# A two-network forward pass on one core: the latent attention's prelude taken block by block, its shared rope key computed as 64 extra columns of the query latent, and the squares of the feed-forward's first groups placed ahead of weight splits

## Chip, cores and metric

The kernel runs on one core of a Trainium2 chip. The metric is the device time of one execution in microseconds (us); lower is better.

## What is computed

Two small networks run one after the other on x of shape 256 x 1024 in float32. The first has a short-convolution mixer and a multi-head latent attention (MLA), each followed by a squared-ReLU feed-forward, all with layer norms; the second a gated linear recurrence and a block attention. The part around the change, shortened:

```python
cq = _rms_norm(x @ w_dq, g_q)                       # 256 x 384, the query latent
q = (cq @ w_uq).reshape(bsz, seq, MLA_HEADS, QK_NOPE + QK_ROPE)
ckv_full = x @ w_dkv                                # 256 x 320
ckv = _rms_norm(ckv_full[..., :KV_LORA], g_kv)      # 256 x 256, the key and value latent
k_pe = _rope(ckv_full[..., None, KV_LORA:], cos, sin)[:, :, 0, :]   # 64 wide, shared by 8 heads
k_nope = jnp.einsum("bsc,chd->bshd", ckv, w_uk)
v = jnp.einsum("bsc,chd->bshd", ckv, w_uv)
...
s = (q_nope . k_nope + q_pe . k_pe) * scale, masked; softmax; times v; @ w_o
...
_sq_relu_mlp: jnp.square(jax.nn.relu(x @ w1)) @ w2  # 1024 -> 4096 -> 1024
```

## The kernel before

**Weights.** Every weight matrix is cut into pieces of at most 128 x 2048 floats (`piece_table`). SyncE's queue (SP) loads them one after another into a ring of three raw buffers (`RAW`), and a load starts when VectorE (DVE) has finished with the piece three places back (`raw_done`). ScalarE (ACT) rounds a piece to the high half (`w_high`, L908), DVE subtracts to get the low half (`w_low`, L1206), both into a ring of six (`RING`); TensorE (PE) then makes each product of three matmuls: high x high, high x low, low x high. `split_ahead(key, n)` on ACT and on DVE carries this on up to n pieces past the piece `key`; where it stands in an engine's program fixes what is queued behind it. Between the weight pieces of a feed-forward lie "mod" pieces of the second network's modulation: DVE accumulates each in eight steps (L1218, L1221), POOL adds the two halves (L862), PE sums over partitions (`mod_sums`, L615), DVE reads the result (`read_mod`, L1231).

**Feed-forward** (`feed_forward`, one function per engine; ff0 and ff1). There are 16 groups of 256 hidden columns; group g is an up product, relu on ACT (L971), the square on DVE (L1348), and two down products, one per block of 128 tokens (b = 0, 1). The first three groups (`FILL`) are made token-major, block 0 first, so that they can begin while block 1's layer norm is still under way: PE runs `up_block(g, 0)` for g = 0, 1, 2, then for each g `up_block(g, 1)` and, from g = 1, `turn(g - 1)`, four transposes that wait for the square of group g - 1 (L533). Then `mod_sums`, the down products of group 0, turn(2), `mod_sums`, and the first feature-major up product, up(3) (L482). On DVE before the change each group starts with `split_ahead((phase, "up", g), AHEAD)`, and the square comes behind it.

**Prelude of the latent attention** (`latents`, L1446 to L1515 on DVE). For each block, PE makes the key-value latent (24 matmuls of 256 columns, piece dkv) and the query latent (24 of 384, pieces dq). The shared rope key is a product of its own: piece kpe holds the 64 columns and their halves exchanged, each twice, and `feature_block` (L510 to L512) multiplies it feature-major, 48 matmuls of 128 columns per block. Block 0's half stands behind the transposes of x's block 1, block 1's half behind the transposes of the key latent (tkv). DVE normalises both blocks of a latent in one go, PE transposes it, DVE applies the gain, ACT and DVE make its high and low half. Then follow keys, the turned query latent, keys, values (`across`), and the attention loop: for each pair of heads the projections qn and qp (36 matmuls of 256 columns), scores (L656, L659), softmax, values. POOL makes the reciprocal roots (L854, L855). Products go through three PSUM banks in the order of `unit_table`; a bank is reopened once it is emptied (`await_evacuated`).

Of the kernel before, what the change touches and what calls it, by code (L numbers as in the profile page):

```python
# [18 lines left out]
ALU = mybir.AluOpType  # L19
# [37 lines left out]
def piece_table():  # L57
# [81 lines left out]
def unit_table():  # L139
# [3 lines left out]
    def attention(phase, projections):  # L143
        for g in range(MXG + 1):
            if g < MXG:
                t.extend((phase, kind, g) for kind in projections)
            if phase == "mo" and g == MXG:
# [7 lines left out]
    t.extend([("mla", "tkv"), ("mla", "kpe"), ("mla", "k", 0), ("mla", "k", 1)])  # L155
    t.extend([("mla", "tq", 0), ("mla", "tq", 1), ("mla", "k", 2), ("mla", "k", 3)])
    t.extend(("mla", "v", b, n) for b in range(TB) for n in range(2))
# [36 lines left out]
def last_unit(phase, kind, n):  # L194
# [5 lines left out]
    return {"kpe": ("mla", "kpe"), "uk": ("mla", "k", 3), "uv": ("mla", "v", 1, 1),  # L200
# [4 lines left out]
LAYER_NORMS = {"ln0": TB, "ln1": TB, "latent": 2, "ln2": TB, "ln3": TB}  # L205
SQUARES = {"rs1": TB, "rs2": TB, "rs3": TB}

ROOTS = {"ln0": TB, "ln1": TB, "latent": 2, "ln2": TB, "ln3": 2 * TB, "rs2": TB, "rs3": TB}
# [51 lines left out]
def build(nc, weights, x_in, cols_in, consts_in, rows_in, out):  # L260
    with ExitStack() as ctx:
# [87 lines left out]
        gain_in, shift_in = sem("gain_in"), sem("shift_in")  # L349
        ones_ready, c_tanh, lam_exp_in, lam_exp = sem("ones_ready"), sem("c_tanh"), sem("lam_exp_in"), sem("lam_exp")  # L350
        prm_ready, diag_ready = sem("prm_ready"), sem("diag_ready")
        lora_ready, lora_high, lora_low, rope_ready = sem("lora_ready"), sem("lora_high"), sem("lora_low"), sem("rope_ready")
# [47 lines left out]
        area_v = area_f.rearrange("p (b n) -> p b n", b=TB)  # L400
        q_all = flat(rows).rearrange("p (h s) -> p h s", s=SEQ)
# [12 lines left out]
        def _(sp):  # L414
# [7 lines left out]
            for s, (kind, n) in enumerate(STREAM):  # L422
# [7 lines left out]
                if s == RAW:  # L430
                    sp.dma_start(consts[:, P:], consts_in[:, P:]).then_inc(consts_in_done, 16)
# [19 lines left out]
        def _(pe):  # L451
# [47 lines left out]

            def feature_block(dst, n, b, fresh):  # L500

                await_piece(n)
                for tile in range(GT):
                    o = dst[:, tile * SEQ + b * P:tile * SEQ + (b + 1) * P]
                    for kt in range(KT):
                        if tile == 0 and kt % 4 == 0:
                            await_xT(fresh, b, kt // 4)
                        c = (tile * KT + kt) * P
                        high, low = w_high[:, n % RING, c:c + P], w_low[:, n % RING, c:c + P]
                        mm(o, high, xT_h[:, kt, tok(b)], start=kt == 0, stop=False)  # L510
                        mm(o, high, xT_l[:, kt, tok(b)], start=False, stop=False)
                        last = mm(o, low, xT_h[:, kt, tok(b)], start=False, stop=kt == KT - 1)  # L512
                return last
# [198 lines left out]
            def latents(b):  # L712

                for q in range(2):
                    await_xT("ln1", b, q)
                i = PI["mla", "dkv", 0]
                await_piece(i)
                token_major(Y[b][1][:, 0:KV_LORA], i, KT, KV_LORA, 0, KV_LORA, b, xT_h, xT_l, True, True).then_inc(latent, 1)
                for n in range(2):
                    i = PI["mla", "dq", n]  # L720
                    await_piece(i)
                    last = token_major(Y[b][0][:, 0:Q_LORA], i, KT // 2, Q_LORA, 0, Q_LORA, b, xT_h[:, 4 * n:4 * n + 4, :],
                                       xT_l[:, 4 * n:4 * n + 4, :], n == 0, n == 1)
                last.then_inc(latent, 1)

            latents(0)
# [990 lines left out]
```

## Time and profile before

| | |
|---|---|
| median of 3 runs | 889.57 us (887.39 to 889.62) |
| profiled execution, its own time | 888.67 us |
| its span in the trace | 886.9 us |
| PE busy | 819.4 us, 92% of the span |
| DVE, ACT, POOL busy | 619.5, 402.1, 156.3 us |
| mean granted TensorE clock | 0.963 |
| moved by DMA | 174.38 MB, mean 197 GB/s |

The span is what the trace covers; the execution's own time is 1.8 us longer. Durations below are from this one profiled execution. In the trace ff0 begins at about 107 us, the prelude at 304.95, the attention's first score at 349.00, and ff1 at about 417. A matmul's duration in the trace overlaps its neighbours', so PE's pace is read from starts. The granted clock is 1.00 at 2.4 GHz and 0.50 at 1.2 GHz.

### The profile page before, as it was taken

The page shows a single profiled execution, that of the slowest core. Times are in us where ns is not written, and L with a number is a line of the kernel's source. Part 1 is how long each engine was busy: PE and PEld are TensorE (multiplying, and loading weights), DVE is VectorE, ACT ScalarE, POOL GpSimd, SP SyncE. Part 2 cuts the span into 40 slices and gives each one's busy share as a digit, 9 for nine tenths or more (in the row PEclk, how much of TensorE's full clock was granted, in tenths as well). Part 3 has the DMA queues.
Part 4 walks back from the last instruction along what each step waited for, and adds up shares of the span by engine and source line. Part 5 has one row for each costly group of instructions (what it writes and reads, how often), then busy time and mean ns, then how long its engine had stood idle before and what let it go on. Part 6 is the DMA issues. An engine that isn't in the chain of part 4 may idle for free.

```text
span 886.9 us, 13139 instructions
## 1 busy us (share of the span) xinstructions
PE 819.4 (92%) x5410; PEld 751.0 (85%) x5410; DVE 619.5 (70%) x941; ACT 402.1 (45%) x469; POOL 156.3 (18%) x86
## 2 busy tenths in 40 slices
PE   6999979999999999999799999997778969979985
PEld 6999878999999897878789999996778959979974
DVE  6776887777777766766877777776477775546643
ACT  5443244434344235561544444343567874454531
POOL 0110012233443000000123344331300002020000
PEclk9999999999999999999999999999798988999998
DMA  7974456877776324333568777762043443734101
GB/s 294 346 284 161 173 196 250 315 283 285 274 272 241 141 72 168 141 143 143 213 241 310 280 285 281 263 244 90 25 167 130 193 171 115 276 137 144 48 25 47
DMA packets 25691, 174.38 MB, mean 197 GB/s; under 512 B 2848, under 2 KB 3104, under 8 KB 6176
## 3 DMA queue, kind: packets, MB, share of 16 engines
q1 hardware_dynamic: 25632, 173.54, 53.4%
q8 instruction: 43, 0.70, 0.3%
q14 instruction: 16, 0.13, 0.0%
HBM read 172.48 MB, written 1.05 MB: 196 GB/s over the span
## 4 chain that ended last, share of the span: by engine, by line
PE 80%; DVE 9%; ACT 6%; DMA 2%; issue 2%; POOL 0%; POOLq 0%; ACTq 0%; SPq 0%; DVEq 0%
PE bank L482 13%; PE bank L484 12%; PE bank L483 12%; PE Y L580 10%; PE Y L581 9%; PE Y L583 9%; DVE w_low L1206 3%; ACT w_high L908 2%; DMA raw<-weights 1%; PE mbank L615 1%; PE Y L606 1%; PE Y L656 1%; PE bank L544 1%; PE bank L545 1%; PE bank L546 1%
## 5 line engine op out<-in xcount | busy, mean ns | idle before, releaser
L1206 DVE TENSOR_TENSOR w_low<-raw,w_high 128x2048 fp32r<-128x2048 f32 (+2 forms) x130 | 287.0, 2227 | 57.0 <-ACT w_high L908 56.4
L482 PE MATMUL bank<-xT_h,w_high 128*128 128x256 f32 x928 | 270.3, 291 | 16.8 <-DVE xT_l L1302 7.2
L908 ACT CAST w_high<-raw 128x2048 fp32r<-128x2048 f32 (+2 forms) x130 | 239.4, 1854 | 80.5 <-DMA raw<-weights 70.9
L483 PE MATMUL bank<-xT_l,w_high 128*128 128x256 f32 x928 | 266.3, 287 | 0.0
L484 PE MATMUL bank<-xT_h,w_low 128*128 128x256 f32 x928 | 266.0, 287 | 0.0
L482 PEld LDWEIGHTS bank<-xT_h,w_high 128*128 128x128 f32 x928 | 181.6, 196 | 18.7 <-issue 8.0
L483 PEld LDWEIGHTS bank<-xT_l,w_high 128*128 128x128 f32 x928 | 181.8, 196 | 0.4 <-issue 0.2
L484 PEld LDWEIGHTS bank<-xT_h,w_low 128*128 128x128 f32 x928 | 181.7, 196 | 0.0
L580 PE MATMUL Y<-w_high,hT_h 128*128 128x512 f32 x344 | 136.7, 397 | 0.2 <-DVE hT_l L1237 0.2
L581 PE MATMUL Y<-w_low,hT_h 128*128 128x512 f32 x344 | 135.5, 394 | 0.0
L583 PE MATMUL Y<-w_high,hT_l 128*128 128x512 f32 x344 | 107.8, 395 | 0.0
L862 POOL TENSOR_TENSOR macc<-macc 128x256 f32<-128x256 f32 x16 | 61.3, 3832 | 153.3 <-DVE macc L1221 153.3
L862 POOL TENSOR_TENSOR stage<-stage 128x256 f32<-128x256 f32 x16 | 63.5, 3970 | 134.5 <-DVE stage L1221 134.5
L971 ACT ACTIVATE buf_a<-bank 128x512 f32<-128x512 f32 x32 | 19.1, 598 | 131.0 <-PE bank L484 124.4
L583 PEld LDWEIGHTS Y<-w_high,hT_l 128*128 128x128 f32 x344 | 65.2, 189 | 14.3
L580 PEld LDWEIGHTS Y<-w_high,hT_h 128*128 128x128 f32 x344 | 65.7, 191 | 13.1 <-DVE hT_l L1237 0.7
L581 PEld LDWEIGHTS Y<-w_low,hT_h 128*128 128x128 f32 x344 | 65.4, 190 | 13.2
L854 POOL TENSOR_SCALAR small<-small 128x1 f32<-128x1 f32 (+1 forms) x16 | 7.1, 444 | 390.7 <-DVE small L1263 171.3
L1348 DVE SCALAR_TENSOR_TENSOR buf_b<-bank,buf_a 128x512 f32<-128x512 f32 x32 | 22.1, 690 | 58.0 <-ACT buf_a L971 58.0
L920 ACT CAST hT_h<-buf_b 128x512 fp32r<-128x512 f32 x34 | 21.1, 620 | 53.1 <-DVE buf_b L1445 28.3
L1221 DVE SCALAR_TENSOR_TENSOR stage<-raw,cs,stage 128x256 f32<-128x256 f32 x96 | 39.4, 480 | 0.0
L1221 DVE SCALAR_TENSOR_TENSOR macc<-raw,cs,macc 128x256 f32<-128x256 f32 x96 | 39.3, 479 | 0.0
(196 smaller groups left out, 1129.3 us busy)
## 6 DMA issues: line engine op xcount, KB each, us to landing
raw<-weights SPq DMA_DIRECT2D x152, 1024.0 KB, 5.1
rows<-rows_in SPq DMA_DIRECT2D x9, 512.0 KB, 7.1
raw<-weights SPq DMA_DIRECT2D x6, 768.0 KB, 4.3
raw<-weights SPq DMA_DIRECT2D x4, 512.0 KB, 4.6
x<-x_in SPq DMA_DIRECT2D x2, 512.0 KB, 4.1
out<-x SPq DMA_DIRECT2D x2, 512.0 KB, 2.7
consts<-consts_in SPq DMA_DIRECT2D x1, 320.0 KB, 5.3
cols<-cols_in SPq DMA_DIRECT2D x1, 118.5 KB, 6.4
```

The lines of the kernel that those rows point to most:

```text
L482: mm(dst, high, xh[:, kt, :], start=kt == 0, stop=False)
L483: mm(dst, high, xl[:, kt, :], start=False, stop=False)
L484: last = mm(dst, low, xh[:, kt, :], start=False, stop=kt == kts - 1)
L580: mm(Y[b][h][:, :], th[:, t0 + t, tok(b)], high[h], start=first, stop=False)
L581: mm(Y[b][h][:, :], th[:, t0 + t, tok(b)], low[h], start=False, stop=False)
L583: last = mm(Y[b][h][:, :], tl[:, t0 + t, tok(b)], high[h], start=False, stop=final)
L862: nc.gpsimd.tensor_tensor(acc[:, 0, :], acc[:, 0, :], acc[:, 1, :], ALU.add).then_inc(mod_added, 1)
L908: nc.scalar.copy(w_high[:, n % RING, start:COLS[n]], raw[:, s % RAW, start:COLS[n]]).then_inc(w_high_ready, 1)
L920: nc.scalar.copy(hT_h[:, t0:t0 + GT, :], src).then_inc(hidden_high, 1)
L1206: tt(w_low[:, n % RING, start:COLS[n]], slot[:, start:COLS[n]], f32(w_high[:, n % RING, start:COLS[n]]), ALU.subtract).then_inc(raw_done, 1)
L1221: step = stt(out=acc, in0=part, scalar=cs[:, kt:kt + 1], in1=acc, op0=ALU.mult, op1=ALU.add)
L1348: squared = stt(out=buf_b[:, g % 2, :], in0=bank_of(phase, g)[:, :], scalar=0.0, in1=buf_a[:, g % 2, :], op0=ALU.max, op1=ALU.mult)
```

## The change

Three parts.

1. **Rope key.** Piece kpe and `feature_block` go. The 64 rope columns are appended to the query latent's weights: the dq pieces are 4 x (384 + 64) columns, and their matmuls 448 wide. DVE turns the key token-major from PSUM (`rope_key`, five small operations per block, with cos and sin per token that one more DMA puts into buf_a), PE transposes it (one transpose per block), ACT copies it.
2. **Prelude by block.** Norm, transposes, gain, high and low half are made per block and interleaved with the latent products; values of block 0 come ahead of the keys, values of block 1 behind the first projections; the piece uv comes before uk.
3. **Feed-forward, groups 0 to 2, in ff0 and ff1.** On DVE and ACT the splits come behind the relu and square of the group; at group 1 only the mod piece is accumulated there, and the two weight pieces wait for group 2.

```diff
     for n in range(2):
-        add("mla", "dq", n, KT // 2 * Q_LORA)
-    add("mla", "kpe", 0)
+        add("mla", "dq", n, KT // 2 * (Q_LORA + ROPE))
+    add("mla", "uv", 0)
     add("mla", "uk", 0)
-    add("mla", "uv", 0)
...
+                if key == ("mla", "uk", 0):
+                    await_evacuated(sp, "ff0", FFG - 1)
+                    sp.dma_start(buf_a[:, 1, 2 * P:], consts_in[:, 2 * P + 2 * SEQ:]).then_inc(key_turn_in, 16)
...
+            latent_kv(0)
+            latent_q(0, 0)
+            transposes("ln1", x, "x_ready", [1])
+            latent_q(0, 1)
+            latent_kv(1)
+            turn_latent("tkv", 0)
+            latent_q(1, 0)
+            turn_latent("tq", 0)
+            latent_q(1, 1)
+            turn_latent("tkv", 1)
+            pe.wait_ge(lora_low, 1)
+            latent_values(0)
+            pe.wait_ge(lora_low, 3)
+            for n in range(4):
+                up(PI["mla", "uk", 0], ("mla", "k", n), 2 * n, CT, *ckv)
+                if n == 1:
+                    turn_latent("tq", 1)
+                    dst = open_unit("mla", "kpe")
+                    for b in range(TB):
+                        pe.wait_ge(kpe_ready, b + 1)
+                        last = nc.tensor.transpose(dst[:, tok(b)], macc[:, b, P:2 * P], ident)
...
             def project(g):
+                if g == 0:
+                    pe.wait_ge(lora_low, 4)
                 for i, kind in enumerate(("qn", "qp")):
                     up(PI["mla", "q", g], ("mla", kind, g), GT * i, QT, hT_h, hT_l)
+                if g == 0:
+                    latent_values(1)
...
             def feed_forward(phase, m0):
                 for g in range(FFG):
-                    split_ahead((phase, "up", g), AHEAD if g else AHEAD - 1)
+                    if g == 0 or g >= FILL:
+                        split_ahead((phase, "up", g), AHEAD if g else AHEAD - 1)
...
+                    if g < FILL:
+                        split_ahead((phase, "up", 0 if g < FILL - 1 else g), AHEAD, min(g, 1) if g < FILL - 1 else 0)
```

**DVE, groups 0 and 1 of ff0** (L1348, after the change L1372, is the square; L1206 and L1226 a weight's low half; raw to stage a mod piece). Before:

```order
L1348 SCALAR_TENSOR_TENSOR buf_b<-bank,buf_a 128x512 [waits relu]
L1206 TENSOR_TENSOR w_low<-raw,w_high 128x2048 [waits w_high_ready]
L1218 TENSOR_SCALAR stage<-raw,cs 128x256 [waits mod_summed,raw_in0]
L1218 TENSOR_SCALAR stage<-raw,cs 128x256
L1221 SCALAR_TENSOR_TENSOR stage<-raw,cs,stage 128x256 [waits dve_chain] x6
L1206 TENSOR_TENSOR w_low<-raw,w_high 128x2048 [waits w_high_ready]
L1348 SCALAR_TENSOR_TENSOR buf_b<-bank,buf_a 128x512 [waits relu]
L1252 TENSOR_TENSOR hT_l<-bank,hT_h 128x512 [waits hidden_high]
```

After the change:

```order
L1372 SCALAR_TENSOR_TENSOR buf_b<-bank,buf_a 128x512 [waits relu]
L1226 TENSOR_TENSOR w_low<-raw,w_high 128x2048 [waits w_high_ready]
L1372 SCALAR_TENSOR_TENSOR buf_b<-bank,buf_a 128x512 [waits relu]
L1272 TENSOR_TENSOR hT_l<-bank,hT_h 128x512 [waits hidden_high]
L1238 TENSOR_SCALAR stage<-raw,cs 128x256 [waits mod_summed,raw_in0]
L1238 TENSOR_SCALAR stage<-raw,cs 128x256
L1241 SCALAR_TENSOR_TENSOR stage<-raw,cs,stage 128x256 [waits dve_chain] x6
L1251 TENSOR_TENSOR modcol<-mbank,cols 128x2 [waits mod_summed]
```

Two weight splits stood between the squares of groups 0 and 1, with a mod piece between them; one split stands there now, and the mod piece follows the second square.

**PE, the transposes of x's block 1 in the prelude** (L606, now L596; x_ready is the layer norm's signal). Before, the rope key's first matmuls follow, with a wait for the transposed block:

```order
L606 MATMUL Y<-consts,x 128x128 [waits x_ready]
L606 MATMUL Y<-consts,x 128x128 x3
L606 MATMUL Y<-consts,x 128x128 [waits x_ready]
L606 MATMUL Y<-consts,x 128x128 x3
L510 MATMUL bank<-xT_h,w_high 128x128 [waits xT_low,raw_done,evacuated2]
L511 MATMUL bank<-xT_l,w_high 128x128
```

After the change:

```order
L536 MATMUL Y<-w_high,xT_l 128x448
L596 MATMUL Y<-consts,x 128x128 [waits x_ready]
L596 MATMUL Y<-consts,x 128x128 x3
L596 MATMUL Y<-consts,x 128x128 [waits x_ready]
L596 MATMUL Y<-consts,x 128x128 x3
L534 MATMUL Y<-w_high,xT_h 128x448 [waits raw_done]
```

What follows the transposes is the second half of block 0's query latent, which waits for its weights alone.

**DVE, the key-value latent's norm and gain** (BN_STATS to the reciprocal root's operand, then the normalised latent buf_b, then the gain from a PSUM bank). Before, in one go for both blocks:

```order
L1462 BN_STATS small<-Y 128x6 [waits latent] x2
L1465 BN_AGGR small<-small 128x2 [waits dve_chain]
L1465 BN_AGGR small<-small 128x2
L1467 TENSOR_TENSOR small<-small 128x2 [waits dve_chain]
L1468 TENSOR_TENSOR small<-small 128x2 [waits dve_chain]
L1474 TENSOR_SCALAR buf_b<-Y,small 128x256 [waits rstd_ready]
L1474 TENSOR_SCALAR buf_b<-Y,small 128x256
L1492 TENSOR_SCALAR stage<-bank,cols 128x256 [waits product]
L1492 TENSOR_SCALAR stage<-bank,cols 128x256
```

After the change, block 0's part (L1330 makes x's low half of block 1, L1226 splits the piece uk):

```order
L1482 BN_STATS small<-Y 128x6 [waits latent]
L1483 BN_AGGR small<-small 128x2 [waits dve_chain]
L1484 SCALAR_TENSOR_TENSOR small<-small 128x1 [waits dve_chain]
L1330 TENSOR_TENSOR xT_l<-Y,xT_h 128x4x128 [waits xT_high] x2
L1491 TENSOR_SCALAR buf_b<-Y,small 128x256 [waits rstd_ready,consts_in_done]
L1226 TENSOR_TENSOR w_low<-raw,w_high 128x2048 [waits w_high_ready]
L1482 BN_STATS small<-Y 128x6 [waits latent]
L1483 BN_AGGR small<-small 128x2 [waits dve_chain]
L1484 SCALAR_TENSOR_TENSOR small<-small 128x1 [waits dve_chain]
L1499 TENSOR_SCALAR buf_b<-bank,cols 128x128 [waits product]
L1499 TENSOR_SCALAR buf_b<-bank,cols 128x128
```

A latent's steps for block 0 now stand ahead of, and between, the steps for block 1.

## Rows read from the trace of the kernel before

**Rows 1.** The page of the profile, part 1 (busy time of PE) and part 4 (the chain).
```profile
PE 819.4 (92%) x5410; PEld 751.0 (85%) x5410; DVE 619.5 (70%) x941; ACT 402.1 (45%) x469; POOL 156.3 (18%) x86
...
PE 80%; DVE 9%; ACT 6%; DMA 2%; issue 2%; POOL 0%; POOLq 0%; ACTq 0%; SPq 0%; DVEq 0%
```

**Rows 2.** PE's waits: line, what was waited for: us in total, times, longest us.
```profile
PE bank L533 <- DVE buf_b L1348: 11.8, 2, 6.4
```

**Rows 3.** Timeline of PE, start of ff0: start us, us, engine, line, operation, tiles.
```profile
131.77 1.11 PE L533 MATMUL bank<-consts,buf_b 128*128 128x128 f32 x4 [6.44 <-DVE buf_b L1348]
...
140.93 0.36 PE L482 MATMUL bank<-xT_h,w_high 128*128 128x256 f32 x1
```

**Rows 4.** Timeline of DVE and ACT, start of ff0 (idle before and its releaser in brackets).
```profile
128.82 2.29 DVE L1206 TENSOR_TENSOR w_low<-raw,w_high 128x2048 fp32r<-128x2048 f32 x1 [2.03 <-ACT w_high L908]
131.03 0.68 DVE L1348 SCALAR_TENSOR_TENSOR buf_b<-bank,buf_a 128x512 f32<-128x512 f32 x1
...
126.89 1.90 ACT L908 CAST w_high<-raw 128x2048 fp32r<-128x2048 f32 x1 [5.32 <-DMA raw<-weights]
```

**Rows 5.** Stretches: us, busy of PE, PEld, DVE, ACT, POOL; granted clock; DMA share; GB/s.
```profile
130.00:135.00 5.00, 3.23 (x12) 2.94 (x13) 5.00 (x6) 2.65 (x3) 0.00 (x0) 0.50 0.75 264
349.00:354.88 5.88, 5.88 (x17) 3.16 (x17) 5.84 (x5) 0.00 (x0) 0.00 (x0) 0.66 0.53 189
354.88:360.42 5.54, 5.54 (x38) 5.54 (x38) 2.80 (x13) 3.79 (x10) 0.00 (x0) 0.74 0.96 356
362.95:367.03 4.08, 4.08 (x19) 2.27 (x17) 3.83 (x11) 1.50 (x5) 0.00 (x0) 1.00 0.48 147
367.03:371.24 4.21, 4.21 (x38) 4.21 (x38) 1.95 (x9) 3.02 (x8) 0.00 (x0) 1.00 0.27 111
```

**Rows 6.** Timeline of PE, start of ff1.
```profile
441.24 1.11 PE L533 MATMUL bank<-consts,buf_b 128*128 128x128 f32 x4 [5.41 <-DVE buf_b L1348]
...
450.94 0.36 PE L482 MATMUL bank<-xT_h,w_high 128*128 128x256 f32 x1
```

**Rows 7.** Timeline of PE: a turn, and two down products with their modulation sum.
```profile
121.86 0.60 PE L533 MATMUL bank<-consts,buf_b 128*128 128x128 f32 x4
122.22 0.36 PE L523 MATMUL bank<-w_high,xT_h 128*128 128x256 f32 x1
...
456.78 0.39 PE L580 MATMUL Y<-w_high,hT_h 128*128 128x512 f32 x1
...
462.27 0.50 PE L615 MATMUL mbank<-ones,stage 128*128 128x1 f32 x4
462.64 0.36 PE L482 MATMUL bank<-xT_h,w_high 128*128 128x256 f32 x1
```

**Rows 8.** The two stretches in which PE computes the shared rope key.
```profile
312.94:318.33 5.39, 5.39 (x50) 5.39 (x49) 3.92 (x4) 4.35 (x4) 0.00 (x0) 1.00 0.49 147
325.79:331.18 5.39, 5.39 (x52) 5.39 (x50) 4.07 (x11) 2.00 (x2) 1.26 (x2) 1.00 0.01 3
```

**Rows 9.** Timeline of PE: latents of block 0, its neighbours, the first score.
```profile
304.95 0.28 PE L544 MATMUL Y<-w_high,xT_h 128*128 128x256 f32 x1
...
307.81 0.34 PE L544 MATMUL Y<-w_high,xT_h 128*128 128x384 f32 x1
...
311.98 0.38 PE L606 MATMUL Y<-consts,x 128*128 128x128 f32 x2
...
349.00 0.46 PE L656 MATMUL Y<-kT,rows 128*128 128x128 f32 x2 [1.42 <-issue]
```

**Rows 10.** Timeline of DVE: around POOL's reciprocal root of the key latent.
```profile
322.40 0.16 DVE L1468 TENSOR_TENSOR small<-small 128x2 f32<-128x2 f32 x1
...
323.67 0.88 DVE L1474 TENSOR_SCALAR buf_b<-Y,small 128x256 f32<-128x256 f32 x2 [1.10 <-POOL small L855]
```

**Rows 11.** Timeline of ACT and POOL: a value bank emptied, a modulation sum's first step.
```profile
343.51 0.59 ACT L1046 COPY z<-bank 128x512 f32<-128x512 f32 x1 [0.76 <-PE bank L546]
...
269.60 4.92 POOL L862 TENSOR_TENSOR stage<-stage 128x256 f32<-128x256 f32 x1 [6.77 <-DVE stage L1221]
```

More of the change, by code:

```diff
@@ L755, in _, with turn_latent @@
-            for b in range(TB):
+            def turn_latent(kind, b):
+                src, kts, count = (ckvn, CT, 2 * b + 1) if kind == "tkv" else (cqn, QT, 2 * b + 2)
+                dst = open_unit("mla", kind, b)
+                pe.wait_ge(lora_ready, count)
+                for kt in range(kts):
+                    last = nc.tensor.transpose(dst[:, kt * P:(kt + 1) * P], src[:, b, kt * P:(kt + 1) * P], ident)
+                in_order("mla", kind, b)
+                last.then_inc(product, 1)
@@ L1047, in _ @@
                         .then_inc(evacuates("mla", "v", b, n), 1)
-            split_ahead(("mla", "uv", 0))
+            latent_high("tkv", 0)
+            split_ahead(("mla", "q", 0), 0)
+            latent_high("tq", 0)
+            latent_high("tkv", 1)
+            latent_values(0)
+            keys(0)
+            keys(1)
+            latent_high("tq", 1)
+            await_product(act, "mla", "kpe")
+            nc.scalar.copy(area[:, 4, :], bank_of("mla", "kpe")[:, 0:SEQ]).then_inc(evacuates("mla", "kpe"), 1)
+            keys(2)
+            keys(3)
+            split_ahead(("mla", "q", 2), 0)
             for g in range(MXG + 1):
@@ L1190, in f32, with split_ahead @@
                 return ap.bitcast(F32)
-            def split_ahead(key, ahead=AHEAD):
-                stop = AT["w", min(PI[key] + ahead, len(PIECES) - 1)]
+            def split_ahead(key, ahead=AHEAD, mods=0):
+                stop = AT["w", min(PI[key] + ahead, len(PIECES) - 1)] + mods
+                assert all(kind == "mod" for kind, _ in STREAM[stop - mods + 1:stop + 1])
                 while done[0] <= stop:
@@ L1470, in latent_normed, with latent_squares @@
-            def latent_normed(i, normed, half, width):
-                await_rstd("latent", i)
-                for b in range(TB):
-                    last = ts(normed[:, b, :], Y[b][half][:, 0:width], rstd[:, TB * i + b:TB * i + b + 1], None, ALU.mult)
-                last.then_inc(lora_ready, 1)
-            def rope(n, *key):
+            def latent_squares(i, b):
+                n, src = TB * i + b, Y[b][0][:, 0:Q_LORA] if i else Y[b][1][:, 0:KV_LORA]
+                dve.wait_ge(latent, 2 * b + i + 1)
+                link(nc.vector.bn_stats(stats[:, n, 0:6], src))
+                link(nc.vector.bn_aggr(mv[:, n, :], stats[:, n, 0:6]))
+                stt(out=msq[:, n:n + 1], in0=mv[:, n, 0:1], scalar=mv[:, n, 0:1], in1=mv[:, n, 1:2], op0=ALU.mult, op1=ALU.add)\
+                    .then_inc(S["var_ready"], 1)
@@ new lines, in latent_low, with rope_key @@
+            def latent_low(i, b):
+                dve.wait_ge(lora_high, 2 * b + i + 1)
+                t0, kts, src = (0, QT, stage[:, b, 0:QT * P]) if i else (QT, CT, buf_b[:, 1, b * CT * P:(b + 1) * CT * P])
+                tt(hT_l[:, t0:t0 + kts, tok(b)], src.rearrange("p (t s) -> p t s", t=kts), f32(hT_h[:, t0:t0 + kts, tok(b)]),
+                   ALU.subtract).then_inc(lora_low, 1)
+            def rope_key(b):
+                k, half = Y[b][0][:, Q_LORA:Q_LORA + ROPE], ROPE // 2
+                straight, crossed = macc[:, b, 0:ROPE], macc[:, b, ROPE:2 * ROPE]
+                dve.wait_ge(latent, 2 * b + 2)
+                dve.wait_ge(key_turn_in, 16)
+                tt(straight, k, cos_k[:, b, :], ALU.mult)
+                tt(crossed[:, 0:half], k[:, half:], sin_k[:, b, 0:half], ALU.mult)
+                link(tt(crossed[:, half:], k[:, 0:half], sin_k[:, b, half:], ALU.mult))
+                for n in range(2):
+                    last = tt(macc[:, b, P + n * ROPE:P + (n + 1) * ROPE], straight, crossed, ALU.add)
+                last.then_inc(kpe_ready, 1)
```

216 lines of the change are left out of this document (92 added, 124 removed).

## The prediction

> **What bounds the kernel now.** I read the page first. PE is busy for 92% of the span, and the chain that ended last lies on PE for 80% of it [rows 1]. So two things can shorten the run: less work on PE, and fewer or shorter waits of PE. The waits by line come next: the largest entry in a feed-forward is L533, the turn of a group in the fill, which waited 11.8 us for the square of DVE in two places [rows 2]. The timelines show where.
>
> In ff0 the second turn starts at 131.77 after 6.44 us of idleness [rows 3]. What it waits for is the square of group 1 at 131.03 on DVE, behind a weight split that started at 128.82. That split waited for ACT's high half, and ACT for a load, 5.32 us [rows 4]. The square is a 0.68 us instruction with its inputs ready long before (the relu of group 1 needs only up products that had ended by 121.9 [rows 7]); it is late because of what is queued ahead of it. While PE stood still its clock fell: the granted clock was 0.50 from 130 to 135 [rows 5], that is 1.2 GHz. ff1 repeats it, with 5.41 us of idleness [rows 6].
>
> In the prelude PE never stands still until the first score at 349.00, where it idles for 1.42 us [rows 9]. The prelude is bound by PE's work, and two stretches of 5.39 us are the rope key's product, at full clock with PE busy throughout [rows 8]. Behind the idle 1.42 us the clock fell again: the scores took 5.88 us and the next projections 5.54 us at a mean clock of 0.66 and 0.74, against 4.08 and 4.21 us in the next round at 1.00 [rows 5].
>
> **The change, term by term.** I sum against the profiled execution's own 888.67 us, which lies 0.9 us under the median of 889.57.
>
> *Feed-forward fill, ff0.* DVE's order becomes: square 0 (about 120), one split (its ACT half is no longer behind a relu, and its load was issued long before), square 1, the low half of group 0, the mod piece, square 2, then two splits. A split takes 2.29 us [rows 4], so square 1 ends near 123.5, before PE asks for it at 131.77 - 6.44 = 125.33 [rows 3]. The mod piece then ends near 127, square 2 near 128. From 125.33 PE now runs straight on: turn 0.36 (122.22 - 121.86), modulation sum 0.37, two down products 5.49 (462.27 - 456.78), turn 0.36, sum 0.37 (462.64 - 462.27) [rows 7], so up(3) starts at 132.28 where it started at 140.93 [rows 3]: 8.65 us gained, 6.44 of it the wait and 2.2 the slow clock behind it. *ff1* likewise: 441.24 - 5.41 + 6.95 = 442.78 against 450.94 [rows 6], 8.16 us. What is late next is the second modulation sum: its mod piece ends near 127, and POOL's add took up to 4.92 us [rows 11], so it is there by 132 and is wanted at 131.9; I take 0.3 us of wait over both. The weight splits put off are two, of group 2's round. Their pieces down(1) and up(4) are wanted by PE at about 138 and 144; with loads issued as slots come free they are split by 134. The slack behind the fill hides them; if it were gone each would cost its 2.29 us. Fill terms: 8.65 + 8.16 - 0.3 = 16.5 us.
>
> *Rope key on PE.* Removed: 2 x 5.39 = 10.78 us, 96 matmuls [rows 8]. Added: 48 of the 128x384 matmuls become 448 wide. The pace is (307.81 - 304.95)/24 = 0.119 us at 256 columns and (311.98 - 307.81)/24 = 0.174 at 384 [rows 9], so 64 columns are 0.027 us, times 48 is 1.3 us. Two transposes at (312.94 - 311.98)/8 = 0.12 us [rows 8, 9] are 0.24. All other PE work of the prelude is only moved. Net 9.2 us. These rows give 0.112 us to a kpe matmul of 128 columns, almost what 256 columns cost. The Trainium skill (TensorE: Matmul & The Clock Gate, Back-to-back issue gap) has a sustained pace of about 81 ns at 128 columns. By that figure the 96 removed matmuls were worth 7.8 us and the sum would be 3.0 us less, near 863.6. The trace has this very work and differs, so the rows decide.
>
> *Waits in the prelude.* The 10.8 us also hid things: block 0's half covered the casts of x's block 1, block 1's half the gain and low half of the key latent. Their new covers, from 304.95: the key latent of block 0 takes 2.9 us, half the query latent 2.4, so PE asks for x's block 1 near 310.2; layer norm gives it at 310.7 (DVE is unchanged up to there): 0.4 us of wait. The other half query latent (2.4) and then the reader of x's low half: the casts need about 2 us behind the transposes, just covered. Query latent, block 0: statistics can start only when its second half ends near 313.6 and stand behind a 2.3 us split; then POOL's root, 1.1 us from request to use (323.67 - 322.40 less the instruction) [rows 10], so it is normalised near 319.5, and PE asks at about 319.0: 0.5 us. Keys need block 1's key latent low at about 325.2, and PE gets there at 325.4. The last query latent's low half comes near 331 and is wanted at 332. The rope key leaves DVE near 327 and is wanted at 329. The rope of the first projection (formerly the 1.42 us) is now covered by block 1's values; instead scores wait until ACT has emptied the last value bank, 0.59 us for the copy [rows 11] and 0.06 to start. Sum of new waits 1.6 us, old wait 1.4. So the first score comes 9.2 + 1.4 - 1.6 = 9.0 us earlier against its predecessor, at 340.0 before the fill's gain.
>
> Bounds for the waits: at best the 0.4 and 0.5 vanish, 0.9 us better; at worst each of the four handovers (query latent block 0, keys, last query latent, first score) is a further 1.1 us root or a 2.3 us split late, about 6 us.
>
> *SP and small operations.* SP gets one more wait and one 128 x 256 load, ahead of q's loads; what it waits for (the last square of ff0) is done some 4 us before. The ten small rope operations, about 0.2 us each, lie on DVE in gaps; they are in the times above. DMA moves 0.8 MB less, on nobody's path.
>
> *The clock at the scores.* The wait ahead of them falls from 1.42 to 0.65 us. The slow stretch cost (5.88 - 4.08) + (5.54 - 4.21) = 3.1 us [rows 5]. Between the attention's later rounds PE idles 0.33 us each time and stays at 1.00; 0.65 is nearer to that, so I let the clock stay up. DVE was busy all of the 5.88 us [rows 5] with splits, so softmax then shows by about 0.5 us: 2.6 us gained. Ends: 0 and 3.1.
>
> Sum: 16.5 + 9.0 + 2.6 = 28.1; 888.67 - 28.1 = **860.6 us**.
>
> **Rivals.**
> A. *The clock still falls at the scores.* For it: PE still idles there, amid small matmuls. Against it: the idle time is halved. 888.67 - 25.5 = 863.2. Chance 0.20.
> B. *The latents' chain is late.* The steps DVE, POOL, DVE, PE, DVE, ACT, DVE now run four times, strictly in DVE's order, so one late step delays all behind it. The margins above are 0.2 us at the keys and 1 us at the last query latent. At 4 to 6 us of waits the time is 865 to 867. Chance 0.18.
> C. *The fill's wait only moves.* The splits put off make down(1), up(4) or the next pieces late, as ACT waited 5.32 us for a load [rows 4]. PE would have to be caught before 144 with half of the gain lost: 860.6 + 8.2 = 869. Against it: six microseconds of slack. Chance 0.08.
> D. *Slower.* The rope product kept PE dense; without it the prelude is short groups between transposes and waits, and the clock could sit at 0.50 from the first latent to the first score. All 33.4 us of work would take 33.4 us more: 860.6 + 33.4 = 894. It decides against the change once some 28 us of full-clock work run at half. Against it: the transposes of x at 311.98 stand in a stretch at 1.00. The Trainium skill (same page, Part 4: PE-mode transpose) holds that transposes don't count as activity for the clock as matmuls do, which speaks for it; no row here shows the clock falling at transposes alone. Chance 0.02.
> E. *The change does not act*, since the square would wait for something else, or the removed product was hidden: within 0.3% of 889. The rows above speak against it. Chance 0.01.
>
> **How the numbers follow.** Forecast 0.51, A 0.20, B 0.18, C 0.08, D 0.02, E 0.01. The mean granted clock of the whole run, 0.963, says that some 65 us ran at half; those other low stretches, of 3 us and more, may shift when everything before them moves, by some 2 us either way at each of a few places. So the forecast's own range is 857 to 863.5. The range of 856 to 868 takes in A and most of B and leaves out C, D and E and the tails. 0.3% is 2.7 us, about what a measurement tells from no change. Faster 0.96, same 0.02, slower 0.02.
>
> **What would show it.** Right: PE's waits for the square gone from the list or under 1 us; up(3) of ff0 near 132.3 and the granted clock 1.00 there; from the first latent to the first score 35.0 us, where it was 44.05; scores of the first round in 4.1 us. Wrong: waits of PE at the latents' transposes, keys or projections of over 1 us each (B); PE idle in groups 3 to 5 of ff0 behind a weight split (C); a granted clock of 0.50 inside the prelude (D). The forecast fails as a whole if the distance from up(3) to the end of a feed-forward grows by what the fill gained.

## The result

The changed kernel takes 862.52 us (median of 4 runs, 860.01 to 863.31), the kernel before 889.6 beside it (4 runs, 887.39 to 891.24). The ratio is 0.9692 with a 95% interval of 0.9663 to 0.9722: some 27 us faster. The prediction was 860.6 us, range 856 to 868.

| | before | after |
|---|---|---|
| profiled execution, its own time | 888.67 | 860.01 |
| span | 886.9 | 858.2 |
| PE busy | 819.4, 92% | 803.0, 94% |
| DVE, ACT, POOL busy | 619.5, 402.1, 156.3 | 618.8, 401.4, 136.8 |
| mean granted TensorE clock | 0.963 | 0.972 |
| matmuls | 5410 | 5316 |

The page of the profile after, parts 1 and 4, where [rows 1] stood:

```profile
PE 803.0 (94%) x5316; PEld 735.4 (86%) x5316; DVE 618.8 (72%) x950; ACT 401.4 (47%) x470; POOL 136.8 (16%) x90
...
PE 84%; DVE 7%; ACT 6%; issue 2%; DMA 0%; POOL 0%; POOLq 0%; ACTq 0%; SPq 0%; DVEq 0%
```

The busy times of DVE and ACT are nearly what they were; more of POOL's adds were short (last section). PE has 94 matmuls less (96 fewer for the key, two more for its transposes), and its waits for the squares are gone. I cut both traces at the same matmuls of PE and compare the parts; every number is the difference of two starts in the PE timeline.

| from, to (us) | before | after | gained |
|---|---|---|---|
| ff0's first up_block to up(3): the fill | 34.31 | 25.77 | 8.54 |
| up(3) to the first latent: rest of ff0 | 164.02 | 164.03 | 0.0 |
| first latent to first score: prelude | 44.05 | 34.14 | 9.91 |
| first score to the next round's: round 1 | 13.95 | 13.99 | 0.0 |
| to ff1's first up_block: rest of attention | 54.16 | 52.56 | 1.60 |
| ff1's fill | 33.83 | 25.76 | 8.07 |
| rest of ff1, to its norm | 164.81 | 164.79 | 0.0 |

Their sum is 28.1 us; 0.6 more lies before and behind them, which makes the 28.7 between the spans. The round of the attention is the stretch from one pair of heads' first score to the next pair's. Nothing was given back in what follows a fill: the rest of a feed-forward takes the same time to 0.02 us.

**The fill.** Timeline of PE in the profile after, with [rows 3, 6] to set beside it: the second turn of ff0 (L523) and up(3) (L487), then the same two of ff1.

```profile
124.82 0.60 PE L523 MATMUL bank<-consts,buf_b 128*128 128x128 f32 x4
...
132.02 0.36 PE L487 MATMUL bank<-xT_h,w_high 128*128 128x256 f32 x1
...
415.31 0.60 PE L523 MATMUL bank<-consts,buf_b 128*128 128x128 f32 x4
...
422.50 0.36 PE L487 MATMUL bank<-xT_h,w_high 128*128 128x256 f32 x1
```

No bracket: PE came without a wait, where it had stood 6.44 and 5.41 us. Timelines of DVE and of ACT at that place, against [rows 4]:

```profile
119.57 0.68 DVE L1372 SCALAR_TENSOR_TENSOR buf_b<-bank,buf_a 128x512 f32<-128x512 f32 x1
120.17 2.28 DVE L1226 TENSOR_TENSOR w_low<-raw,w_high 128x2048 fp32r<-128x2048 f32 x1
122.37 0.68 DVE L1372 SCALAR_TENSOR_TENSOR buf_b<-bank,buf_a 128x512 f32<-128x512 f32 x1
```
```profile
121.70 0.60 ACT L980 ACTIVATE buf_a<-bank 128x512 f32<-128x512 f32 x1 [2.28 <-PE bank L515]
...
135.46 1.91 ACT L916 CAST w_high<-raw 128x2048 fp32r<-128x2048 f32 x1 [4.89 <-DMA raw<-weights]
```

The square of group 1 begins at 122.37, right behind one split and its relu, and 8.66 us sooner than before (8.29 if both are counted from the start of the fill). The relu at 121.70 stands behind PE's product and behind no load. ACT still waits 4.89 us for a load, but at 135.46, where the engines behind it have pieces in hand. The load's lateness was not removed; it was moved to where nothing needs it.

Stretches of the profile after, where [rows 5] stood: the fill, then the first round's scores and projections, then the next round's scores (columns as there).

```profile
130.00:135.00 5.00, 5.00 (x39) 4.71 (x39) 4.98 (x9) 0.57 (x1) 0.00 (x0) 1.00 0.78 283
330.19:335.72 5.53, 5.53 (x16) 2.95 (x16) 4.19 (x4) 3.03 (x2) 0.00 (x0) 0.72 0.88 286
335.72:341.64 5.92, 5.92 (x37) 5.92 (x37) 3.05 (x13) 3.78 (x10) 0.00 (x0) 0.69 0.73 291
344.18:348.25 4.07, 4.07 (x18) 2.26 (x16) 3.81 (x11) 1.50 (x5) 0.00 (x0) 1.00 0.47 137
```

The fill runs at 1.00 where it was 0.50. The first scores do not: in this execution their clock fell as it did in the profile before, and round 1 gained nothing.

**The prelude.** One stretch over the whole of it, first the profile before, then the profile after:

```profile
304.95:349.00 44.05, 42.61 (x319) 40.84 (x318) 28.22 (x50) 18.64 (x21) 2.90 (x6) 1.00 0.34 116
```
```profile
296.05:330.19 34.14, 33.24 (x225) 30.68 (x224) 26.37 (x58) 14.50 (x21) 3.99 (x10) 1.00 0.27 94
```

PE's work fell by 42.61 - 33.24 = 9.37 us, its idle time from 1.44 to 0.90. And its timeline:

```profile
298.90 0.37 PE L534 MATMUL Y<-w_high,xT_h 128*128 128x448 f32 x1
...
301.34 1.11 PE L596 MATMUL Y<-consts,x 128*128 128x128 f32 x8
302.21 0.45 PE L534 MATMUL Y<-w_high,xT_h 128*128 128x448 f32 x1
...
310.26 0.49 PE L728 MATMUL bank<-consts,buf_a 128*128 128x128 f32 x3
...
330.19 0.46 PE L646 MATMUL Y<-kT,rows 128*128 128x128 f32 x2 [0.77 <-ACT z L1050]
```

The one bracket is the first score's, which waits 0.77 us for the last value bank; the other 0.13 us of idleness stands ahead of the keys behind the key's transposes. The 448-column matmuls run at (301.34 - 298.90)/12 = 0.203 us each. The eight transposes of x's block 1 took 0.87 us (302.21 - 301.34), in a prelude whose granted clock is 1.00 throughout. The Trainium skill (TensorE: Matmul & The Clock Gate, Part 4: PE-mode transpose) does not count these as activity for the clock; nothing in this prelude shows a cost of that.

### The profile page after: what moved, and what is told of

It is laid out like the page before. It is cut to its first block, busy times and chain, and to the rows that moved or that the text cites. A ratio compares the mean times of both kernels' runs of the same rounds, so it can differ in the third digit from the quotient of the medians.

```text
span 858.2 us, 12965 instructions
## 1 busy us (share of the span) xinstructions
PE 803.0 (94%) x5316; PEld 735.4 (86%) x5316; DVE 618.8 (72%) x950; ACT 401.4 (47%) x470; POOL 136.8 (16%) x90
## 4 chain that ended last, share of the span: by engine, by line
PE 84%; DVE 7%; ACT 6%; issue 2%; DMA 0%; POOL 0%; POOLq 0%; ACTq 0%; SPq 0%; DVEq 0%
PE bank L487 13%; PE bank L489 13%; PE bank L488 13%; PE Y L570 10%; PE Y L573 10%; PE Y L571 10%; ACT w_high L916 2%; DVE w_low L1226 2%; PE Y L596 1%; PE bank L513 1%; PE bank L515 1%; PE bank L514 1%; PE mbank L605 1%; PE bank L534 1%; PE Y L646 1%
## 5 line engine op out<-in xcount | busy, mean ns | idle before, releaser
L1226 DVE TENSOR_TENSOR w_low<-raw,w_high 128x2048 fp32r<-128x2048 f32 (+2 forms) x129 | 285.4, 2230 | 66.9 <-ACT w_high L916 66.2
L487 PE MATMUL bank<-xT_h,w_high 128*128 128x256 f32 x928 | 270.0, 291 | 16.8 <-DVE xT_l L1322 7.1
L487 PEld LDWEIGHTS bank<-xT_h,w_high 128*128 128x128 f32 x928 | 181.3, 195 | 18.8 <-issue 8.0
L868 POOL TENSOR_TENSOR macc<-macc 128x256 f32<-128x256 f32 x16 | 59.5, 3720 | 165.5 <-DVE macc L1241 165.5
L860 POOL TENSOR_SCALAR small<-small 128x1 f32<-128x1 f32 x18 | 7.3, 406 | 377.6 <-DVE small L1283 164.5
L868 POOL TENSOR_TENSOR stage<-stage 128x256 f32<-128x256 f32 x16 | 44.8, 2802 | 126.0 <-DVE stage L1241 126.0
L1372 DVE SCALAR_TENSOR_TENSOR buf_b<-bank,buf_a 128x512 f32<-128x512 f32 x32 | 22.0, 687 | 35.7 <-ACT buf_a L980 35.6
L1257 DVE TENSOR_TENSOR hT_l<-buf_b,hT_h 128x512 fp32r<-128x512 f32 x34 | 23.5, 692 | 22.1 <-ACT hT_h L928 22.0
```

Of the source, the lines that this page charges most:

```text
L487: mm(dst, high, xh[:, kt, :], start=kt == 0, stop=False)
L868: nc.gpsimd.tensor_tensor(acc[:, 0, :], acc[:, 0, :], acc[:, 1, :], ALU.add).then_inc(mod_added, 1)
L1226: tt(w_low[:, n % RING, start:COLS[n]], slot[:, start:COLS[n]], f32(w_high[:, n % RING, start:COLS[n]]), ALU.subtract).then_inc(raw_done, 1)
L1257: tt(hT_l[:, t0:t0 + GT, :], src, f32(hT_h[:, t0:t0 + GT, :]), ALU.subtract).then_inc(hidden_low, 1)
L1372: squared = stt(out=buf_b[:, g % 2, :], in0=bank_of(phase, g)[:, :], scalar=0.0, in1=buf_a[:, g % 2, :], op0=ALU.max, op1=ALU.mult)
```

## The experiments

All ratios are to the kernel before, run on the same chip beside the experiment. The parts of the table above were read from each experiment's profile too.

**Each half alone.** `e1_fill_alone` is the kernel before with the new places of the splits on ACT and DVE, `e2_prelude_alone` the changed kernel with the old places. The diff of e1 on ACT:

```diff
-                    split_ahead((phase, "up", g), AHEAD if g else AHEAD - 1)
+                    if g == 0 or g >= FILL:
+                        split_ahead((phase, "up", g))
...
+                    if g == FILL - 1:
+                        split_ahead((phase, "up", g))
```

and on DVE:

```diff
-                    split_ahead((phase, "up", g), AHEAD if g else AHEAD - 1)
+                    if g == 0 or g >= FILL:
+                        split_ahead((phase, "up", g), AHEAD if g else AHEAD - 1)
...
+                    if g < FILL:
+                        split_ahead((phase, "up", 0 if g < FILL - 1 else g), AHEAD, min(g, 1) if g < FILL - 1 else 0)
```

> The kernel before with only the new place of the splits in groups 0 to 2, on ACT and DVE. Theory (the terms add up): PE's two waits for the square, 6.4 and 5.4 us, and the slow clock behind them go; 16.5 us faster, about 873, first score 8.6 us earlier, prelude itself unchanged at 44.05 us from first latent to first score. Rival C (the wait only moves): PE idle behind a weight split in groups 3 to 5, half of the gain, about 881.

> The changed kernel with the splits of groups 0 to 2 put back ahead of the squares. Theory (the terms add up): the two waits at the turns come back, the prelude stays at about 34 us from first latent to first score, so 10 to 11.5 us faster than the kernel before, about 878. Rival (the prelude only gains because the earlier fill left the weights further ahead of PE): under 6 us faster, with waits of PE for w_low inside the prelude.

Measured: e1 870.64 us against 888.83, ratio 0.9797 (0.9769 to 0.9824), 18 us faster; its fills are 25.75 and 25.77 us, its prelude 43.95. e2 877.58 us, ratio 0.9873 (0.9846 to 0.9900), 11 us faster; prelude 34.23, fills 34.27 and 33.45. Each half does its own part of the time and leaves the other's alone. The two gains add to 29 us where both together give 27; intervals of 2 to 3 us allow that. There is also something else in both: the profiles of e1 and e2 have a round 1 of 12.25 and 12.19 us, with the clock at 1.00, where those of the kernel before and of the changed kernel have 13.95 and 13.99. So e1's fills account for 8.56 + 8.06 = 16.6 of its 18 us.

**DVE's order without ACT's.** `e3_dve_fill_order_alone` has the DVE half of e1's diff and not the ACT half.

> The kernel before with DVE's new order in groups 0 to 2, ACT's order left: the relu of group 1 stays behind the high half of down(1), which waits for its load. If DVE's own queue is what made the square late, the full 16.5 us come, about 873. If ACT's queue holds the relu just as long, the square of group 1 moves only from 131.0 to about 129.5 in ff0 and likewise in ff1: 2 to 4 us faster, about 886.

Measured: 885.07 us, ratio 0.9955 (0.9939 to 0.9971), 4 us faster against e1's 18. Timelines of ACT, DVE and PE in this experiment:

```profile
127.16 1.90 ACT L908 CAST w_high<-raw 128x2048 fp32r<-128x2048 f32 x1 [4.94 <-DMA raw<-weights]
128.97 0.59 ACT L971 ACTIVATE buf_a<-bank 128x512 f32<-128x512 f32 x1
```
```profile
129.59 0.69 DVE L1350 SCALAR_TENSOR_TENSOR buf_b<-bank,buf_a 128x512 f32<-128x512 f32 x1 [5.04 <-ACT buf_a L971]
```
```profile
130.34 0.90 PE L533 MATMUL bank<-consts,buf_b 128*128 128x128 f32 x3 [4.36 <-DVE buf_b L1350]
```

DVE is now free and waits 5.04 us for the relu, which stands on ACT behind a cast that waited 4.94 us for its load. The same load holds the same turn through the other queue. The two fills (33.51 and 32.64 us) gained only 2.0 us between them; most of the rest of the 4 us is, in the profile, a round 1 of 12.25 us for 13.95. DVE's order alone is thus worth an eighth of what both are. ACT's order alone was not run.

**The change again.** `a1_after_again` and `a2_after_again` are the changed kernel unaltered, each run beside other experiments on its chip.

> The changed kernel unchanged, as the measure for the three that are built on it and run beside it. 862 us; first score at about 34.1 us from the first latent; a low clock just behind it.

> The changed kernel once more, beside the next one that is built on it: 862 to 863 us. Its first attention round (first score to first score of the next round) 13.0 or 14.0 us, by where the low clock falls.

Measured: 862.67 us, ratio 0.9702 (0.9678 to 0.9726), and 861.94, 0.9692 (0.9672 to 0.9713). Their parts agree with those of the first profile to 0.05 us in the fills, the rest of ff0 and the prelude. Round 1 does not: 13.05 and 12.17 us, against 13.99. The low clock that I expected just behind the first score of the first repeat did not come there, and the second repeat's round lies below the 13.0 or 14.0 us expected of it. Stretches of the second repeat, the scores and what follows them:

```profile
331.16:335.24 4.08, 4.08 (x16) 2.34 (x16) 2.77 (x2) 3.03 (x2) 0.00 (x0) 1.00 0.89 301
335.24:343.33 8.09, 6.67 (x51) 6.08 (x51) 7.43 (x19) 4.97 (x12) 0.00 (x0) 1.00 0.68 256
```

Here the clock stayed at 1.00 and the scores took 4.08 us; but PE was busy for 6.67 of the 8.09 us behind them. The first repeat, whose clock also was up until 342.3, shows what filled the rest. Timelines of DVE, ACT and PE:

```profile
333.81 2.29 DVE L1226 TENSOR_TENSOR w_low<-raw,w_high 128x2048 fp32r<-128x2048 f32 x1 [0.35 <-ACT w_high L916]
...
336.26 0.29 DVE L1393 TENSOR_REDUCE small<-Y 128x1 f32<-128x128 f32 x1
```
```profile
339.12 1.90 ACT L916 CAST w_high<-raw 128x2048 fp32r<-128x2048 f32 x1
340.91 0.87 ACT L1003 COPY buf_b<-bank 128x384 f32<-128x384 f32 x2
```
```profile
339.67 0.52 PE L660 MATMUL bank<-consts,buf_a 128*128 128x128 f32 x3 [0.21 <-DVE buf_a L1400]
...
341.54 0.67 PE L669 MATMUL bank<-buf_b,z 128*128 128x256 f32 x2 [1.35 <-ACT buf_b L1003]
```

Softmax starts at 336.26 behind a 2.29 us split, and ACT's copies at 340.91 behind a 1.90 us one; PE waits 0.21 and 1.35 us for them. In the first profile after, with the clock down, PE's only wait behind the first score of the round was 0.33 us: a slow PE hides these waits, a fast one meets them.

**The rope product put back as dead work.** `e4_key_work_back` adds two sets of 48 matmuls of 128 columns to the changed kernel, where the key's product had stood, into unused columns of mbank; nothing reads them.

```diff
             transposes("ln1", x, "x_ready", [1])
+            dead_product(0)
             latent_q(0, 1)
...
             turn_latent("tkv", 1)
+            dead_product(1)
```

> The changed kernel with 2 x 48 matmuls of 128 columns, the shape and count of the old rope key product, put back as dead work into unused PSUM columns: 48 behind the transposes of x's block 1, 48 behind the last transposes of the key latent. Theory (PE-bound prelude, 0.112 us each): 10.8 us slower less the waits that they cover (at most 0.5), so 10.3 to 10.8 over the changed kernel, about 873. By the page's 81 ns: 7.8 us slower. Rival (they would be hidden by DVE's chain): under 3 us slower.

Measured: 872.27 us, ratio 0.9803 (0.9780 to 0.9827), 9.6 us over the changed kernel beside it; its prelude 44.98 us against 34.18, 10.8 us for 96 matmuls. PE's timeline, first matmul of the first set and the one behind its last:

```profile
302.51 0.31 PE L747 MATMUL mbank<-xT_h,w_high 128*128 128x128 f32 x1
...
307.90 0.42 PE L534 MATMUL Y<-w_high,xT_h 128*128 128x448 f32 x1
```

That is 5.39 us, the figure of [rows 8]: 0.112 us a matmul, not the 81 ns that the prediction took from the Trainium skill to weigh against it. In the new order the product is worth its full length.

**The 64 columns taken away.** `e5_no_key_columns` computes no rope key: the query latent's matmuls are 384 columns wide and the key is made from what lies in the bank.

```diff
-                last = token_major(Y[b][0][:, 0:width], i, KT // 2, width, 0, width, b, xT_h[:, 4 * n:4 * n + 4, :],
+                last = token_major(Y[b][0][:, 0:Q_LORA], i, KT // 2, Q_LORA, 0, width, b, xT_h[:, 4 * n:4 * n + 4, :],
```

> The changed kernel with the query latent's matmuls 384 wide instead of 448: the 64 rope key columns are left out, so the key is not computed. Theory: 48 x 0.027 = 1.3 us less PE work, seen as 1.3 us less from first latent to first score, less what turns into a wait for the query latent's norm (up to 0.5): 0.8 to 1.3 us faster. Rival (columns are free below 512 because the weight load sets the pace): no change in the prelude's length.

Measured: 861.18 us, ratio 0.9694 (0.9671 to 0.9717), against 862.67 of the changed kernel beside it, a difference that the intervals cover; prelude 33.79 us, only 0.4 less where I had expected 0.8 to 1.3. PE's timeline shows where the rest went:

```profile
301.50 1.31 PE L596 MATMUL Y<-consts,x 128*128 128x128 f32 x8
302.56 0.42 PE L534 MATMUL Y<-w_high,xT_h 128*128 128x384 f32 x1
...
310.53 0.52 PE L728 MATMUL bank<-consts,buf_a 128*128 128x128 f32 x3 [0.43 <-DVE buf_a L1491]
```

With the columns PE had arrived just behind the normalised query latent of block 0; without them it waits 0.43 us for it. The transposes of x's block 1 took 1.06 us for 0.87: PE came to them earlier and x did not. And the four halves of the query latents became 1.04 us shorter, that wait aside, and not 1.3. The key's columns thus cost 0.4 us where they stand, and the prelude has little left to give to a cut on PE alone.

**The rope product removed from the old order.** `e8_old_order_no_key` is the kernel before, with an eighth of the key's product: 12 matmuls for 96.

```diff
-                    for kt in range(KT):
+                    for kt in range(kts):
...
-            feature_block(kpe, PI["mla", "kpe", 0], 0, "ln1")
+            feature_block(kpe, PI["mla", "kpe", 0], 0, "ln1", 1)
```

> The kernel before, in its old order, with the rope key's product cut to one eighth (2 x 6 of 2 x 48 matmuls, so the key is wrong): 9.4 us less PE work, about what the change takes away, but no work by block. If the old product was cover for nothing, the prelude is 9.4 us shorter, 34.6 us. Theory (it covered the casts of x's block 1 and the chain of the key latent's norm, and the block order is what replaces that cover): waits of about 2 us at the transposed block and 2 to 3 us at the key latent appear, the prelude is only 4 to 6 us shorter, 38 to 40 us, and the run 4 to 7 us faster than the kernel before.

Measured: 884.47 us, ratio 0.9950 (0.9932 to 0.9967), 5 us faster; prelude 39.52 against 44.05, 4.5 of the 9.4 us that were taken out. PE's timeline:

```profile
315.11 0.36 PE L544 MATMUL Y<-w_high,xT_h 128*128 128x256 f32 x1 [0.82 <-DVE xT_l L1310]
...
326.01 0.39 PE L482 MATMUL bank<-hT_h,w_high 128*128 128x256 f32 x1 [2.56 <-DVE hT_l L1496]
...
332.19 0.39 PE L482 MATMUL bank<-hT_h,w_high 128*128 128x256 f32 x1 [0.87 <-DVE stage L1505]
```

Of the 4.9 us that are missing, 4.25 are new waits: at x's block 1, at the keys, and at the bank of the turned query latent. The order by blocks is not worth much by itself either: e4, which has it together with the full product, has a prelude of 44.98 us against the old 44.05, with 1.3 us of key columns in it. It is what makes the removal pay, for about half of the prelude's gain.

**The moved wait, and the split ahead of the softmax.** `e6_value_wait_later` puts PE's wait for the value banks behind the scores. `e9_split_alone` instead lets ACT and DVE prepare one piece less in each round of the attention; `e7_one_split_less` does both. In e6 and e7, on PE:

```diff
+                if phase == "mla" and heads[0] == 0:
+                    for b, n in ((0, 1), (1, 0), (1, 1)):
+                        await_evacuated(pe, "mla", "v", b, n)
...
-                    for b, n in ((0, 1), (1, 0), (1, 1)):
-                        await_evacuated(pe, "mla", "v", b, n)
```

In e7 and e9, on ACT and on DVE:

```diff
-                    split_ahead(("mla", "q", g))
+                    split_ahead(("mla", "q", g), AHEAD - 1)
```

> The changed kernel with the wait for the emptied value banks taken from the first score to the first product that reads the values, 12 us later. The 0.77 us of idleness before the first score goes. Theory (the clock falls at the scores because PE idled): it stays at 1.00 there, 0.8 + about 3 us faster, 858 to 859. Rival (the scores themselves, small matmuls of full float32, let it fall whatever precedes them): 0.7 us faster and the low clock remains.

> The changed kernel with the value banks' wait moved as in e6 and, in the attention loop, ACT's and DVE's splits kept 3 pieces ahead, not 4, so that the softmax of the first round stands behind one split less (2.3 us). Theory (the first round is held by DVE's splits ahead of the softmax, which is why a high clock there gave little): PE's waits for the first probabilities go, the round falls from 13 to 14 us to about 11.5, and with the 0.9 us of e6 it is 2 to 3.5 us faster than the changed kernel, near 860. Rival (what is taken out there is only paid after the last round, where the pieces of the down products come late): a wait for w_low at the down products, no change.

> The changed kernel with only the splits of the attention loop kept 3 pieces ahead instead of 4; the value banks' wait stays ahead of the first score (0.77 us). If the split ahead of the softmax is what held the first round: round near 11 us where the scores run at full clock, 1 to 3 us faster than the changed kernel (862), and e7's gain is mostly this. If e7's gain came from the moved wait: no change from 862.

> e7 once more on another chip: 0.966 to 0.967 of the kernel before, about 859; a ratio at or above 0.969 would say that its lead over the changed kernel was chance.

| | us | ratio (95%) | prelude | round 1 |
|---|---|---|---|---|
| changed kernel, first repeat | 862.67 | 0.9702 (0.9678 to 0.9726) | 34.18 | 13.05 |
| changed kernel, second repeat | 861.94 | 0.9692 (0.9672 to 0.9713) | 34.12 | 12.17 |
| e6, later wait | 862.60 | 0.9696 (0.9672 to 0.9719) | 33.24 | 14.05 |
| e9, one split less | 859.57 | 0.9677 (0.9661 to 0.9694) | 34.22 | 11.03 |
| e7, both | 858.68 | 0.9664 (0.9641 to 0.9687) | 33.30 | 10.93 |
| e7 again | 859.20 | 0.9676 (0.9658 to 0.9693) | 33.25 | 10.93 |

e6 is a miss: the 0.9 us left the prelude and did not show in the total. Its clock stayed at 1.00 over the scores, as in the first repeat, and fell at 342.3 as there; the 3 us expected from that did not come, since round 1 took 14.05 us all the same. Its timeline of PE has the waits of the first repeat and one more:

```profile
339.20 0.52 PE L660 MATMUL bank<-consts,buf_a 128*128 128x128 f32 x3 [0.84 <-DVE buf_a L1401]
...
341.80 0.69 PE L672 MATMUL bank<-buf_b,z 128*128 128x256 f32 x2 [1.35 <-ACT buf_b L1004]
```

PE came earlier and waited longer. With the split gone from ahead of the softmax (e9), round 1 falls to 11.03 us and its largest wait to a third of a microsecond, PE's timeline of e9:

```profile
339.98 0.67 PE L669 MATMUL bank<-buf_b,z 128*128 128x256 f32 x2 [0.33 <-DVE area L1534]
```

So the split held the round, once the clock was up: e9's scores ran at 1.00 as those of the second repeat did, and its round is 1.1 us shorter. By both its runs e7 is the fastest version found, some 3 us under the changed kernel by the medians; the intervals of the ratios overlap, so that the parts (prelude 0.9 and round 1 at least 1.2 us shorter in each profile) are better evidence for it than the totals are. That the moved wait adds anything beside the split is not shown: e7 again and e9 have the same ratio.

## Why the prediction was right

The time came out within 2 us of 860.6, inside the forecast's own range and the full one. Two of its three terms were right in their mechanism; the third, the clock, was not, and that the sum came out so near is in part luck, as its last items show. Term by term:

- **Fill: right.** Predicted 8.65 and 8.16 less 0.3 for both; measured 8.54 and 8.07. The turns, sums and down products laid end to end put up(3) at 132.28; shifted by ff0's earlier start (106.25 for 106.62) that is 131.91, and it came at 132.02. The 0.3 for the modulation sum was not there as a wait: POOL's add for it, which the prediction put at up to 4.92 us from another place, took 0.74, and 0.72 at the same place of the profile before. e1 shows the term by itself (25.75 and 25.77 us), and e3 that it needs ACT's new order beside DVE's. Rival C (the wait only moves) is out: the rest of each feed-forward is unchanged to 0.02 us.
- **Rope key's work: right.** Predicted 9.2 us net, PE's busy time fell by 9.37. The 7.8 us that the prediction worked out from the Trainium skill's pace were wrong here; e4 measured 10.8. (The DMA moves 0.68 MB less and not 0.8, on nobody's path as was said.)
- **Waits in the prelude: over-estimated by 0.9 us.** The step that failed is "0.4 us of wait" at x's block 1 and "0.5 us" at block 0's query latent. Neither came. For the first, the prediction took 310.7, the end of the layer norm before the change, as the time at which all of x's block 1 is there. But DVE writes x in two halves, and the first four transposes want only the first:

```profile
300.34 1.40 DVE L1296 SCALAR_TENSOR_TENSOR x<-Y,small,rows 128x512 f32<-128x512 f32 x2
```

  (timeline of DVE in the profile after). At 0.70 us a half the first was written near 301.04 and the second near 301.74; PE began at 301.34 and had started its fourth by then. For the second, the query latent was put at 319.5 - 304.95 = 14.55 us into the prelude; in e5 PE had it at 310.53 - 296.40 = 14.13, where the changed kernel asks at 14.21 (310.26 - 296.05). That is how close it is: with e5's columns gone 0.43 us of wait appeared there. The margins named for rival B at the keys and the last query latent held as well; B is out at 0.9 us of idleness in all. The wait ahead of the scores was put at 0.65 and is 0.77.
- **The clock at the scores: the failed step.** "0.65 is nearer to that, so I let the clock stay up ... 2.6 us gained." In the profiled execution it fell, as rival A had it, and round 1 gained nothing. In the second repeat it stayed up through the round, and that was worth 13.99 - 12.17 = 1.8 us and not 2.6: I had let softmax show by 0.5 us, and PE waited 1.42. Nor does the length of the wait decide: e1, e3 and e8 keep the old wait of 1.42 us and the old round, and in all three the clock stayed at 1.00 and round 1 took 12.25 us. There is one profile of the kernel before, so its 13.95 us, from which the term was priced, need not be what that kernel always does. The changed kernel's three profiles, and those of e2 and e4 with the same wait and splits, show a round of 13.99, 13.05, 12.17, 12.19 and 14.01. The fall comes in some executions and not in others; neither forecast nor rival A was the right picture of it, and why it falls stays open.
- **The time of the rest.** The profiled execution gained 1.6 us behind round 1 for a reason that no term held: the profile before has a stretch there at half clock, and this one has none.

```profile
391.90:395.30 3.40, 3.40 (x12) 2.83 (x11) 1.61 (x4) 1.50 (x4) 0.00 (x0) 0.50 1.02 422
```

  (stretch of the profile before). It begins behind waits of 1.45 and 0.21 us; the same place of the profile after has waits of 1.46 and 0.21, and the clock stayed up. The repeats show such a stretch again, near 372, and take 55.16 and 54.15 us for this part. Without the clock at the attention the sum is 8.54 + 9.91 + 8.07 = 26.5 us, and the medians say 27. The forecast's 28.1 had 2.6 us of clock that the profile does not have and lacked 0.9 us of the prelude; the profile's 860.01, nearer to it than the medians, has its 1.6 us from this stretch. That is the luck in it.
- **Slower (D): out.** The prelude stayed at 1.00 from the first latent to the first score, though it is now short groups of matmuls between transposes.

## What to carry to other kernels

When a matrix engine waits for a small vector instruction, look for what is queued ahead of it on every engine of its chain, and move the long, prefetching work behind it on each of them; done on DVE alone it took 2.0 us off the two fills here, on ACT and DVE 16.6. Taking work off the busiest engine pays in full only if what the work hid is moved at the same time: the rope product was worth 10.8 us in the new order (e4, 96 matmuls) and 4.5 in the old (e8, 84 of them). Put no price on a clock that falls in one profile until a second profile of the same kernel shows it again, and count what waits a faster clock would uncover.

## What was not expected of the hardware

- The granted clock at the same instructions of the same kernel differs between executions: 0.72 and 0.69 over the first scores and projections in one, 1.00 in another. This alone moves round 1 by 1.8 us; the runs of one kernel lie 3 to 6 us apart. Why it falls in one and not in the other is open.
- A matmul of 128 columns costs PE 0.112 us and one of 256 columns 0.119 [rows 9]; 384 cost 0.174 and 448 0.203. From 256 to 128 columns nearly nothing was saved. The Trainium skill (TensorE: Matmul & The Clock Gate, Back-to-back issue gap) has about 81 ns at 128 columns; e4 does not bear that out for these operands.
- The same 128x256 add on POOL takes one of three times, in both kernels. The 32 of them took about 0.73 us (2 before, 9 after), 2.7 (11 and 7) or 4.92 (19 and 16), and the switch of some from long to short is the fall of POOL's busy time. Timeline of POOL in the profile after:

```profile
117.52 2.72 POOL L868 TENSOR_TENSOR macc<-macc 128x256 f32<-128x256 f32 x1 [7.43 <-DVE macc L1241]
126.62 0.74 POOL L868 TENSOR_TENSOR stage<-stage 128x256 f32<-128x256 f32 x1 [6.38 <-DVE stage L1241]
...
157.91 4.92 POOL L868 TENSOR_TENSOR macc<-macc 128x256 f32<-128x256 f32 x1 [7.82 <-DVE macc L1241]
```

  The trace's times on POOL are rough. What they depend on was not tried.
